# Twelve shared expert tiles in fp32 column groups instead of sixteen split-precision expert tiles

## The reference, cut to what matters

```python
combine = route(h, w_router, router_bias)      # (512, 16), two nonzero weights per token
for e in range(16):
    a = silu(h @ w_gate[e]) * (h @ w_up[e])    # w_gate, w_up: 1024 x 256
    out = out + combine[:, e:e + 1] * (a @ w_down[e])   # w_down: 256 x 1024
ple = sigmoid(h @ w_ple_gate) * (p @ w_ple_proj)
x = layer_norm(alpha * h + out + ple)
```

## Time and profile before

| | |
|---|---|
| median of 3 runs | 449.11 us (449.06 to 449.18) |
| the profiled execution's own time | 449.11 us |
| its span in the profile | 447.2 us |
| TensorE busy | 430.5 us (96%) |
| VectorE, ScalarE, GpSimd busy | 340.9, 231.6, 107.9 us |
| moved by DMA | 103.16 MB, 231 GB/s over the span |
| expert stage, first gate/up product to last down product | 263.4 to 421.0 us |

### The profile page before, as it was taken

How to read it: one execution, slowest core, us unless ns; L and a number is a source line. 1 busy time by engine, 2 the same in 40 slices (tenths; PEclk the granted TensorE clock), 3 DMA queues, 4 the chain that set the end, 5 groups by cost and what they waited for, 6 DMA issues and landing times.

```text
span 447.2 us, 5541 instructions
## 1 busy us (share of the span) xinstructions
PE 430.5 (96%) x1983; PEld 306.3 (68%) x1983; DVE 340.9 (76%) x533; ACT 231.6 (52%) x371; POOL 107.9 (24%) x142
## 2 busy tenths in 40 slices
PE   7999999999999999999999999999999999999891
PEld 4777664487675557666777876777777777777651
DVE  3999958887748989987585256788777777789677
ACT  4721443151886930216112156788877777889522
POOL 2830288191005300000007410222223222211200
PEclk9999999999999999999999999999999999999997
DMA  8992105224995941113920259999999999840593
GB/s 274 429 376 87 48 14 113 47 79 131 391 424 224 364 158 48 47 47 114 414 86 1 43 188 426 406 420 419 417 378 381 352 374 387 312 202 22 217 222 143
DMA packets 33242, 103.16 MB, mean 231 GB/s; under 512 B 16060, under 2 KB 17260, under 8 KB 26048
## 3 DMA queue, kind: packets, MB, share of 16 engines
q1 hardware_dynamic: 24064, 91.74, 53.5%
q0 software_dynamic: 5600, 9.44, 6.8%
q10 hardware_dynamic: 3552, 1.65, 1.4%
HBM read 95.39 MB, written 17.86 MB: 253 GB/s over the span
## 4 chain that ended last, share of the span: by engine, by line
PE 89%; DVE 5%; ACT 2%; DMA 2%; issue 1%; DVEq 0%; SPq 0%; ACTq 0%
PE bank L1369 9%; PE bank L1172 6%; PE bank L973 6%; PE bank L1341 6%; PE bank L1021 5%; PE bank L1183 5%; PE bank L1346 5%; PE bank L1350 5%; PE bank L1354 5%; PE bank L1256 3%; PE bank L1258 3%; PE bank L1257 3%; PE bank L1325 3%; PE bank L988 2%; PE bank L1013 2%; PE bank L1030 2%
## 5 line engine op out<-in xcount | busy, mean ns | idle before, releaser
L1346 PE MATMUL bank<-gate_up_upper,tokens_upper 128*128 128x512 f32 x96 | 36.3, 459 | 0.0
L1172 PE MATMUL bank<-region_b,region_e 128*128 128x512 f32 x68 | 32.9, 607 | 0.0
L1929 DVE TENSOR_TENSOR gate_up_lower<-region_a,gate_up_upper 128x1024 fp32r<-128x1024 f32 x24 | 28.0, 1220 | 2.6 <-ACT gate_up_upper L893 2.6
L583 POOL DMA_INDIRECT slot_scratch<-region_h,slot_i x8 | 8.9, 1109 | 87.1 <-issue 87.1
L1350 PE MATMUL bank<-gate_up_upper,tokens_lower 128*128 128x512 f32 x96 | 29.8, 392 | 0.0
L596 POOL DMA_INDIRECT expert_scratch<-region_g,region_h x8 | 9.9, 1244 | 79.9 <-ACT region_g L920 79.9
L973 PE MATMUL bank<-region_e,region_a 128*128 128x512 f32 x64 | 28.0, 595 | 0.0
L1256 PE MATMUL bank<-ple_gate_upper,hidden_upper 128*128 128x512 f32 x64 | 25.7, 402 | 0.0
L1346 PEld LDWEIGHTS bank<-gate_up_upper,tokens_upper 128*128 128x128 f32 x96 | 18.1, 189 | 10.4 <-issue 5.7
L1258 PE MATMUL bank<-ple_gate_upper,hidden_lower 128*128 128x512 f32 x64 | 25.0, 390 | 0.0
L1257 PE MATMUL bank<-ple_gate_lower,hidden_upper 128*128 128x512 f32 x64 | 25.0, 390 | 0.0
(11 more groups left out here) (386 smaller groups left out, 1134.1 us busy)
## 6 DMA issues: line engine op xcount, KB each, us to landing
region_a<-in_w_exp_gate SPq DMA_DIRECT2D x8, 1024.0 KB, 8.6
region_a<-in_w_exp_up SPq DMA_DIRECT2D x8, 1024.0 KB, 17.4
region_a<-in_w_exp_down SPq DMA_DIRECT2D x8, 1024.0 KB, 17.4
region_b<-in_w_out SPq DMA_DIRECT2D x1, 4096.0 KB, 15.0
expert_scratch<-zero_scratch SPq DMA_DIRECT2D x8, 512.0 KB, 9.4
region_b<-in_w_exp_gate SPq DMA_DIRECT2D x4, 1024.0 KB, 9.9
region_b<-in_w_exp_up SPq DMA_DIRECT2D x4, 1024.0 KB, 16.9
region_b<-in_w_exp_down SPq DMA_DIRECT2D x4, 1024.0 KB, 17.0
```

The lines of the kernel that those rows point to most:

```text
L1172: last = mm(bank[WO_AT[half][group]][:], hdT[:, k, t * P:(t + 1) * P], w_o[:, k, half * 512:half * 512 + 512], start=(i == 0), stop=(i == ...
L1346: mm(out_, x_hi[r][:, k * P:(k + 1) * P], w_hi[:, k], start=False, stop=False)
L1929: tt(w_lo[:, :, at:at + 2 * DE], w[:, :, at:at + 2 * DE], w_hi[:, :, 2 * c * DE:2 * (c + 1) * DE], ALU.subtract).then_inc(S["gu_lo_set"], 1)
```

## The change

The experts no longer have a tile each. Four experts of a group share three tiles of 128 slots: `members(t)` says that tile 3q holds experts 4q and 4q+1 with 64 slots each, tile 3q+1 all four with 32 each, tile 3q+2 experts 4q+2 and 4q+3 with 64 each. So there are `ET` = 12 tiles, an expert has room for 96 rows, and ten overflow tiles stand behind.

The split into upper and lower parts goes, for gate/up and for down; all products are fp32. In a tile each member multiplies its own 64 or 32 token columns (stationary) with its own weights (moving), k step by k step, and writes its own partitions of the bank by `tile_position`. ScalarE does silu and the copies of results, VectorE the copies of transposed tokens and activations. The weights have five buffers; gate/up and down have separate semaphores. Three tiles are late instead of two, and the scattered results come back by eight plain loads and are added on VectorE. Slots take five more small VectorE steps.

```diff
-KS = 6
-CAP = P
-OVER = 7
-LATE = 2
-SLOT_TILES = NE + OVER
+HOME, MORE = 64, 32
+CAP = HOME + MORE
+ET = 3 * NE // 4
+OVER = 10
+LATE = 3
+WT = 5
...
+def members(t):
+    first = EPG * (t // 3)
+    return ((first, first + 1), tuple(range(first, first + EPG)), (first + 2, first + 3))[t % 3]
...
-        ebuf = [RA[:, 0:6144], RB[:, 0:6144], RA[:, 6144:12288], RC[:, 0:6144]]
+        gu_e = [RA[:, 0:4096], RB[:, 0:4096], RA[:, 6144:10240], RC[:, 0:4096], RH[:, 0:4096]]
+        dn_e = [RA[:, 4096:6144], RB[:, 4096:6144], RA[:, 10240:12288], RC[:, 4096:6144], RA[:, 12288:14336]]
```

SyncE, loads (the first two experts as before; then, behind the wait for `pe_pg`):

```diff
-            load_expert(2, 2)
-            load_expert(3, 3)
+            load_gu(2)
+            load_gu(3)
+            load_dn(2)
+            load_dn(3)
+            load_gu(4)
+            load_dn(4)
...
+            for q in range(3):
+                last = min(EPG * q + 9, NE)
+                sp.wait_ge(S["pe_gu"], 3 * q + 2)
+                for e in range(EPG * q + 5, EPG * q + 7):
+                    load_gu(e)
+                sp.wait_ge(S["pe_gu"], 3 * q + 3)
+                for e in range(EPG * q + 7, last):
+                    load_gu(e)
+                sp.wait_ge(S["pe_dn"], 3 * q + 2)
+                for e in range(EPG * q + 5, EPG * q + 7):
+                    load_dn(e)
+                sp.wait_ge(S["pe_dn"], 3 * q + 3)
+                for e in range(EPG * q + 7, last):
+                    load_dn(e)
...
+            for t in range(NT):
+                if t == NT - 1:
+                    sp.wait_ge(S["pe_gu"], ET - 1)
+                sp.dma_start(y_two[t], yv[t, 1]).then_inc(S[f"y_in{t}"], 16)
+                sp.dma_start(y_one[t], yv[t, 0]).then_inc(S[f"y_in{t}"], 16)
```

TensorE:

```diff
+            def gate_up_rows(out_, x, b, at, width, k):
+                w = gu_e[b].rearrange("p (u k n) -> p k u n", u=2, k=KD)
+                return mm(out_[at:at + width].rearrange("p (u n) -> p u n", u=2), x[:, k, at:at + width], w[:, k],
+                          start=(k == 0), stop=(k == KD - 1), tile_position=(0, at))
...
+            def gate_up(t):
+                group = members(t)
+                width = P // len(group)
+                pe.wait_ge(S["hgT_evac"], 2 * t + 2)
+                if t >= 2:
+                    pe.wait_ge(S["a_ready"], t - 1)
+                for e in group:
+                    pe.wait_ge(S[f"gu_in{e % WT}"], 32 * (e // WT + 1))
+                for k in range(KD):
+                    for j, e in enumerate(group):
+                        last = gate_up_rows(bank[B_GU[t % 2]], hgT[:, t % 2], e % WT, j * width, width, k)
+                last.then_inc(S["pe_gu"], 1)
...
+            tokens_of(0)
             ple_gate(2 * NT - 1)
+            tokens_of(1)
+            for t in range(ET):
+                gate_up(t)
+                if t >= 1:
+                    down(t - 1)
+                if t + 2 < ET:
+                    tokens_of(t + 2)
+                pe.wait_ge(S["a_ready"], t + 1)
+                turn_act(t % 2).then_inc(S["pe_aT"], 1)
+            down(ET - 1, B_TOK, True)
...
+            for t in range(2):
+                for i in range(LATE - 1):
+                    both_halves(t, i)
+            for t in range(2):
+                both_halves(t, LATE - 1).then_inc(S["pe_dn"], 1)
+            for t in range(2, NT):
+                for i in range(LATE):
+                    last = both_halves(t, i)
+                last.then_inc(S["pe_dn"], 1)
```

VectorE and ScalarE:

```diff
+            def add_early(t):
+                dv.wait_ge(S[f"y_in{t}"], 32)
+                link(tt(xh[:, t, :], xh[:, t, :], y_two[t], ALU.add))
+                tt(xh[:, t, :], xh[:, t, :], y_one[t], ALU.add).then_inc(S["one_added"], 1)
...
+            for t in range(ET):
+                gate_times_up(t)
+                if t + 2 < ET:
+                    hgT_copy(t + 2)
+                elif t == ET - 1:
+                    for half in range(2):
+                        late_lower(1, half, B_DN)
+                aT_copy(t)
...
+                if t == ET - 2:
+                    for half in range(2):
+                        late_lower(0, half, B_DN)
+                    add_early(0)
+                    add_early(1)
+            add_early(2)
+            for half in range(2):
+                late_lower(2, half, B_TOK)
+            add_early(3)
...
+            for t in range(ET):
+                ac.wait_ge(S["pe_gu"], t + 1)
+                if t >= 2:
+                    ac.wait_ge(S["a_ready"], t - 1)
+                a.activation(act_e[:, t % 2, 0, :], bank[B_GU[t % 2]][:, 0:DE], ACT.Silu).then_inc(S["silu_done"], 1)
+                if t > ET - LATE:
+                    late_copy(t - 1)
+                elif t >= 1:
+                    y_copy(t - 1)
```

More of the change, by code:

```diff
@@ L423, in _ @@
             load(lnb2, io["ln"][3:4, :].partition_broadcast(P), "ln_in")
[L424 to L430, removed]
@@ L927, in _ @@
-            ac.wait_ge(S["ple_lo_set"], KD + NT)
-            hgT_copy(0, 0)
-            ac.wait_ge(S["pe_pp"], 2 * NT)
-            gate_up_upper(0, 1)
-            ple_gate(2 * NT - 1)
-            for e in range(NE):
-                expert(e, e % 4, e // 4 + 1, last=(e == NE - 1))
-                if 1 <= e < NE - 1:
-                    y_copy(e - 1, (0, 1))
-            ac.wait_ge(S["pe_dn"], NE - 1)
+                             scale=inv_w[:, ET - LATE + i, 1:2]).then_inc(S["yh_set"], 1)
@@ new lines, in down @@
+            def down(t, banks=B_DN, each=False):
+                group = members(t)
+                width = P // len(group)
+                pe.wait_ge(S["aT_evac"], t + 1)
+                if t == 0:
+                    pe.wait_ge(S["ple_done"], 2 * NT)
+                elif t <= ET - LATE:
+                    pe.wait_ge(S["ye_evac"], 2 * t)
+                elif t < ET - 1:
+                    pe.wait_ge(S["yh_set"], 2 * (t - (ET - LATE)))
+                    pe.wait_ge(S["yl_set"], 2 * (t - (ET - LATE)))
+                for e in group:
+                    pe.wait_ge(S[f"dn_in{e % WT}"], 16 * (e // WT + 1))
@@ L1410, in _ @@
-            tokens_of(0, 1)
-            ple_gate(2 * NT - 1)
-            for e in range(4):
-                expert(e, e, 1, first=(e == 0))
-            with pe.Fori(1, NE // 4 - 1) as blk:
-                for b in range(4):
-                    expert(4 * blk + b, b, blk + 1)
-            for e in range(NE - 4, NE):
-                expert(e, e % 4, NE // 4, last=(e == NE - 1))
-            pe.wait_ge(S["aT_hi"], NE)
-            pe.wait_ge(S["dn_lo_set"], NE)
-            down_split(3, 1, dn_hi_last, B_TOK, "pe_dn")
+                        for j, e in enumerate(group):
+                            last = down_rows(half, t % 2, e % WT, j * width, width, k, banks)
@@ L1431, in _ @@
                         pe.wait_ge(S["o_in"], 48 * (o + 1))
-                        gate_up(0, 0).then_inc(S["o_pe"], 1)
+                        for k in range(KD):
+                            last = gate_up_rows(bank[B_GU[0]], hgT[:, 0], 0, 0, P, k)
+                        last.then_inc(S["o_pe"], 1)
                         pe.wait_ge(S["o_vec"], 4 * o + 2)
@@ L1435, in _ @@
                         pe.wait_ge(S["o_act"], 4 * o + 4)
-                        down(0, 0).then_inc(S["o_pe"], 1)
+                        for half in range(2):
+                            for k in range(2):
+                                last = down_rows(half, 0, 0, 0, P, k, B_DN)
+                        last.then_inc(S["o_pe"], 1)
                         pe.wait_ge(S["o_vec"], 4 * o + 4)
@@ L1950, in _, with hgT_copy @@
-            gate_up_lower(0, 0)
-            ple_sum(2 * NT - 1)
-            for e in range(4):
-                step(e, e)
-            with dv.Fori(1, NE // 4 - 1) as blk:
-                for b in range(4):
-                    step(4 * blk + b, b)
+            def hgT_copy(t):
+                dv.wait_ge(S["pe_hgT"], t + 1)
+                for u in range(2):
+                    v.tensor_copy(hgT[:, t % 2, 4 * u:4 * u + 4, :],
+                                  bank[B_TOK[u]][:].rearrange("p (k s) -> p k s", k=4)).then_inc(S["hgT_evac"], 1)
@@ L1975, in _ @@
+            add_early(2)
+            for half in range(2):
+                late_lower(2, half, B_TOK)
+            add_early(3)
+            dv.wait_ge(S["one_added"], NT)
             n_over = dv.value_load(over_i[0:1, 0:1], min_val=0, max_val=OVER)
-            dv.wait_ge(S["ye_out0"], 16 * NE // 4)
+            dv.wait_ge(S["ye_out0"], 16 * 3)
             with dv.If(n_over > 0):
```

396 lines of the change are left out of this document (123 added, 273 removed).

## The result

The changed kernel takes **443.22 us** (median of 4 runs, 441.62 to 443.33); the kernel before, in runs beside them, 449.09 us (448.99 to 449.18). The ratio is 0.9861, 95% interval 0.9838 to 0.9884: 5.9 us less, where 2.5 were forecast. The profiled execution took 443.33 us, its span is 441.6.

What follows compares the result with a forecast made beforehand. TensorE hides an already full DMA stream; once TensorE is cheaper, the load queue bounds. Last up weights land at 391.0, plus 27.9 to the last down's end at 418.9, tail 25.8, and 1.9 outside the span: 446.6 us, range 439 to 452.

Steps and rivals of the forecast that it cites:

- the first reading: Expert stage of the kernel before: SyncE's load queue never runs dry, so 9.9 us an expert is its capacity.
- the TensorE-bound rival: Expert stage: queue faster than 9.9 us an expert, tiles back to back, TensorE sets the end; 439.5 us, chance 0.27.
- k step, 2 and 4 members: Products of a tile: column groups run side by side, so a k step costs 0.86 us whatever its members.
- tile: TensorE's work on one tile of the expert stage: 11.43 us plus 0.4 for group width changes, 11.8 us.
- load queue: Weight loads on SyncE: 9.9 us an expert; gate/up of tiles 4, 7 and 10 wait 1 to 3 us each.
- head: Before the first gather: new VectorE steps take 1.2 us, less 0.5 slack, so 0.7 us; bounds 0 and 1.2.
- tile 1 waits: After tile 0: TensorE waits 3.8 us for tile 1's weights; clock loss taken as 0, bound 2.
- wait before last down: Before down 11: VectorE does late_lower of tile 10 before the needed copy, a 2.7 us wait; bounds 1.5 and 5.
- last down ends: End of the expert stage: last up weights land at 391.0, then 27.9 us of work, so 418.9 us.
- tail: After the last down product: a VectorE chain of combine, centre and scale, 25.8 us instead of 26.2; bounds 24 and 29.
- the column groups: Members' products in a tile: fp32 column groups overlap; the rival without overlap, about 640 or 545 us, had chance 0.03.
- the clock after a wait: TensorE after waiting for tile 1's weights: its clock could fall; taken as 0, bound 2 us.

Runs made afterwards that it cites:

- e3_spread: The kernel before with each expert's slots spread over all 128 partitions, nothing else changed; 449.18 us, ratio 0.9997.
- e1_cut: The kernel before without five of the six gate/up products with the lower part of the weights in each expert; 450.5 us, ratio 1.0023.
- e2_cut_spread: The kernel before with the same products left out as in e1_cut and rows spread over all partitions as in e3_spread; 440.07 us, ratio 0.9792.
- e10_cut_blocks: e1_cut with rows laid in blocks of 32, slots 32 to 63 in partitions 64 to 95 and 64 to 95 in 32 to 63; 442.42 us.
- e4_copy_first: The changed kernel with VectorE copying tile 11's turned activations before making the lower parts of tile 10's result; 440.39 us, ratio 0.9796.
- e6_head: The changed kernel with the seven VectorE steps that count overflow tiles moved later, meant to stand behind the first tile's gather; 444.86 us, ratio 0.9896.
- e5_fill: The changed kernel with three idle fp32 products on TensorE in the wait for tile 1's weights; 442.69 us, ratio 0.9844.
- e8_busy: The changed kernel with eight idle copies a tile on ScalarE and eight on VectorE; 442.8 us, ratio 0.9866.
- e7_all: The changed kernel with the edits of e4_copy_first, e5_fill and e6_head together; 441.91 us, ratio 0.9816.

## Why the prediction was wrong

The step that failed is the first reading: "because a load waits over 16 us throughout, the queue never runs dry: that is its capacity". A queue that is never empty shows its pace under this mix of transfers. What bounded it were eight of the sixteen engines, while the others were done early (the increments under e3_spread, and the dips to 235 GB/s). e1_cut shows the pace for the old layout (10.23 us an expert), e2_cut_spread and e10_cut_blocks that the layout alone makes it 8.97 and 9.15. In the changed kernel, whose tiles fill both halves, the queue gave 419 GB/s and no tile after tile 1 waited for it.

Two readings could have warned me. First, 289 to 325 ran at 418 GB/s and 325 to 395 at 362, both with loads queued; I took the first for the exception and gave the TensorE-bound rival, which came true, 0.27. Second, "over 16 us throughout" is not what the page says of the gate weights:

```profile
region_a<-in_w_exp_gate SPq DMA_DIRECT2D x8, 1024.0 KB, 8.6
region_a<-in_w_exp_up SPq DMA_DIRECT2D x8, 1024.0 KB, 17.4
```

The two are issued 0.4 us apart and count on one semaphore (`e_in`), so the first sixteen of its increments, taken for the landing of gate, can be eight of each load. This fits the lead of one half of the engines again, some 9 us.

| step | forecast | measured |
|---|---|---|
| k step, 2 and 4 members | 0.86 us | 7.02/8 and 7.00/8 = 0.88 |
| tile | 11.8 | 11.86 |
| load queue | 9.9 us an expert, three tiles wait 1 to 3 us | no wait after tile 1, TensorE-bound |
| head | +0.7 | +1.25 (loads issued 264.85, before 263.60) |
| tile 1 waits | 3.8, clock 0 (bound 2) | 3.13, clock +1.8 |
| wait before last down | 2.7 | 2.5, and clock +1.7 |
| last down ends | 418.9 | 415.45 |
| tail | 25.8 | 26.15 |

The span came out 3.1 us below the forecast: 3.45 less up to the last down product, 0.35 more behind it. The product and tile terms were right, and the column groups do run side by side.

Two smaller terms were mis-sized, against the change. The head had a second path: TensorE waited 1.26 us at 241.86 for `ple_proj_lower` on VectorE, behind the slot steps and the larger overflow steps; the forecast counted only slots, write, read, gather. And the clock after a wait was taken as nothing. In the changed kernel it fell 0.9 us after TensorE had resumed from 3.13 us without work: the records' starts lie 0.43 us apart, then some 0.85 from 278.1 to 281.5 (half, so 1.2 instead of 2.4 GHz), then 0.43 again; the earlier trace rows has no such stretch. Without these two falls the span would have been near 438 and the time near 440, beside the rival's 439.5. So the clock, which the forecast put at nothing, brought the time nearer to it, by luck.

One sum was wrong in itself: 263.6 + 10.6 + 1.5 is 275.7, and the 276.4 for the landing of tile 1's weights has the head's 0.7 in it already, which is then added again. The wait should have been 3.0 us, and 3.13 were measured. It bears on the TensorE-bound rival alone (438.8 instead of 439.5). Set against the rival's 411.8 for the end of the last down product, the measured 415.45 is made up of head +0.55, wait -0.67, the two falls +3.5, last wait -0.2, tiles and products +0.5.

That the 5.9 us came from the change's TensorE saving *and* its accidental layout is shown only by the pairs on the kernel before. The changed kernel with its rows back in one half wasn't run: its column groups fix the partitions. At 10.0 to 10.2 us an expert for that layout, against 8.9 of TensorE, tiles would have waited; by the forecast's own 1 us for each tenth of a us the time would have been 447.6 to 449.6 (an estimate).

## What to carry to other kernels

A queue with long latencies shows its pace, not its capacity. Compare GB/s over short slices with the best stretch of the same trace; if it dips while loads are queued, ask which engines the small transfers use, and whether the increments of one load come in two groups of eight. Lay the valid rows of partly filled tiles over both halves of the partitions; it costs a few small instructions, and pays only once the transfers set the time. Before moving small VectorE steps off the path, look at what then stands beside GpSimd's indirect DMAs.

## What was not expected of the hardware

- The same bytes at 367 or 419 GB/s (e1_cut, e2_cut_spread), by the partitions of the gathered and scattered rows alone.
- The sixteen increments of one weight load in two groups of eight, the last 11.7 us after the eighth, in the kernel before; all within 1.8 us in e3_spread.
- TensorE idle for 3.13 us cost a further 1.8 us of half clock (3.0 us in e4_copy_first's profiled run, behind a wait of 3.6 us: 10.01 against 7.00). But 2.5 us idle ahead of the last down product cost 1.7 in two profiled executions (the changed kernel, e6_head) and nothing in two others (e5_fill, e8_busy), and behind 1.82 us in e7_all the clock fell too.
- Eight idle copies a tile on each of two engines left the DMA at 419 GB/s, and the time where it was as far as four runs can tell.
- An indirect DMA's issue on GpSimd grew from 0.97 to 2.53 us beside one VectorE subtraction, but not when it began 0.04 us ahead of it.
